# A feed-forward down product by a seven-product block scheme, in a two-layer float32 transformer block on one core

## What is computed

```python
def _swiglu(h, w_gu, w_down):
    gate, up = jnp.split(h @ w_gu, 2, axis=-1)
    return (jax.nn.silu(gate) * up) @ w_down
...
        h = _rms_norm(x, norm_ffn_pre[l])
        y = _swiglu(h, w_gu[l], w_down[l])
        x = x + _rms_norm(y, norm_ffn_post[l])
```

## Time and profile before

| | |
|---|---|
| time, median of 3 runs | 1101.56 us (1101.35 to 1102.26) |
| span of the profiled execution | 1099.9 us |
| PE busy | 1089.6 us (99%) |
| PEld busy | 1014.0 us (92%) |
| DVE busy | 559.5 us (51%) |
| ACT busy | 561.2 us (51%) |
| POOL busy | 670.2 us (61%) |
| DMA | 183.37 MB, mean 167 GB/s |

### The profile page before, as it was taken

The page is one execution under the profiler, slowest core; times in us unless marked ns, Lnnn a source line. Parts: engine busy times, 40 slices in busy tenths (PEclk is TensorE's granted clock), DMA queues, the critical chain, the costliest instruction groups (busy, mean ns, idle before and its releaser), DMA issues.

```text
span 1099.9 us, 19903 instructions
## 1 busy us (share of the span) xinstructions
PE 1089.6 (99%) x8135; PEld 1014.0 (92%) x8138; DVE 559.5 (51%) x1082; ACT 561.2 (51%) x888; POOL 670.2 (61%) x351
## 2 busy tenths in 40 slices
PE   8999999999999999999999999999999999999997
PEld 7999999998898999999999999999989979999996
DVE  6788479354515631223358866793644344212234
ACT  7645864435655544444464567544356554444442
POOL 4876769627673457654377758685378454586442
PEclk9999999999999999999999999999999999999999
DMA  7443544624543655555555444445155255555553
GB/s 291 173 154 135 188 130 163 180 74 170 194 153 125 205 188 186 180 189 180 184 173 173 157 141 164 152 156 163 69 194 194 97 181 178 191 179 187 187 180 112
DMA packets 63337, 183.37 MB, mean 167 GB/s; under 512 B 18576, under 2 KB 19088, under 8 KB 63248
## 3 DMA queue, kind: packets, MB, share of 16 engines
q1 hardware_dynamic: 47936, 172.48, 45.3%
q10 hardware_dynamic: 15312, 9.64, 3.4%
HBM read 179.47 MB, written 2.62 MB: 166 GB/s over the span
## 4 chain that ended last, share of the span: by engine, by line
PE 97%; ACT 1%; DVE 1%; DMA 1%; POOL 0%; issue 0%; SPq 0%; DVEq 0%; ACTq 0%; POOLq 0%
PE psum L494 28%; PE psum L495 27%; PE psum L496 27%; PE psum L658 1%; PE psum L985 1%; PE psum L964 1%; PE psum L699 1%; PE psum L1086 1%; PE psum L588 1%; PE psum L879 1%; PE psum L872 1%; PE psum L754 1%; DMA sb_raw<-weights 1%; PE psum L682 1%; PE psum L843 0%; PE psum L670 0%
## 5 line engine op out<-in xcount | busy, mean ns | idle before, releaser
L391 POOL TENSOR_TENSOR sb_low<-sb_raw,sb_high 128x1024 fp32r<-128x1024 f32 x257 | 616.5, 2413 | 337.3 <-ACT sb_high L381 323.1
L381 ACT ACTIVATE sb_high<-sb_raw 128x1024 fp32r<-128x1024 f32 x322 | 340.1, 1061 | 406.4 <-DMA sb_raw<-weights 361.6
L494 PE MATMUL psum<-sb_h_high,sb_high 128*128 128x256 f32 x1640 | 463.9, 283 | 0.0
L495 PE MATMUL psum<-sb_h_low,sb_high 128*128 128x256 f32 x1640 | 463.3, 282 | 0.0
L496 PE MATMUL psum<-sb_h_high,sb_low 128*128 128x256 f32 x1640 | 462.5, 282 | 0.0
L494 PEld LDWEIGHTS psum<-sb_h_high,sb_high 128*128 128x128 f32 x1640 | 310.3, 189 | 1.8 <-DVE sb_region_c L1879 0.3
L496 PEld LDWEIGHTS psum<-sb_h_high,sb_low 128*128 128x128 f32 x1640 | 308.6, 188 | 0.0
L495 PEld LDWEIGHTS psum<-sb_h_low,sb_high 128*128 128x128 f32 x1640 | 307.7, 188 | 0.9
L391 DVE TENSOR_TENSOR sb_low<-sb_raw,sb_high 128x1024 fp32r<-128x1024 f32 x65 | 85.4, 1314 | 95.4 <-ACT sb_high L381 95.0
L1992 DVE SCALAR_TENSOR_TENSOR sb_conv<-psum,sb_param,sb_conv 128x255 f32<-128x255 f32 (+1 forms) x144 | 58.2, 473 | 37.0 <-ACT sb_conv L1405 36.8
L2248 DVE SCALAR_TENSOR_TENSOR sb_sq<-sb_th,psum 128x512 f32<-128x512 f32 x22 | 15.1, 687 | 110.0 <-ACT sb_th L1610 110.0
(11 more groups left out here) (307 smaller groups left out, 1549.0 us busy)
## 6 DMA issues: line engine op xcount, KB each, us to landing
sb_raw<-weights SPq DMA_DIRECT2D x322, 512.0 KB, 3.2
sb_pre_gain<-pre_gains ACTq DMA_DIRECT2D x6, 512.0 KB, 4.4
sb_post_gain<-post_gains ACTq DMA_DIRECT2D x6, 512.0 KB, 4.5
sb_kx<-mem SPq DMA_DIRECT2D x2, 512.0 KB, 4.4
sb_x<-x SPq DMA_DIRECT2D x1, 1024.0 KB, 10.7
t_dram<-sb_sq ACTq DMA_DIRECT2D x4, 256.0 KB, 2.9
out<-sb_x SPq DMA_DIRECT2D x4, 256.0 KB, 2.0
m_dram<-sb_m ACTq DMA_DIRECT2D x8, 64.0 KB, 2.1
```

The lines of the kernel that those rows point to most:

```text
L381: nc.scalar.activation(high[:, n % HIGHS, :], raw[:, n % RAWS, :], ACT.Copy).then_inc(high_ready, 1)
L391: eng.tensor_tensor(low[:, k, :], raw[:, k, :], high[:, n % HIGHS, :].bitcast(F32), ALU.subtract).then_inc(low_ready[k], 1)
L494: pe.matmul(out, a[0], b[0], start=start, stop=False, **kw)
L495: pe.matmul(out, a[0], b[1], start=False, stop=False, **kw)
```

## The change

The down product of slots 0 to 9 is written as a 2 x 2 block product: A is 256 tokens by 256 hidden features, in blocks A11, A12, A21, A22 of 128 x 128, and B is 256 hidden features by 1024 outputs, in blocks of 128 x 512. Seven block products of sums of blocks replace the eight. Each of the seven has its own PSUM bank over all ten slots, and the four blocks of the result are put together at the end. Slot 10 (`down_end`) still uses the plain form.

- Sums of A: four 128x128 additions on VectorE (`row_sums`). The operands of slot i are now 8 blocks, 128x1024, rounded on ScalarE (`ff_high`) with the remainder on VectorE (`ff_low`).
- Sums of B, from the raw weights: T1 = B12-B11, T3 = B22-B12, T2 = T3+B11, T4 = B21-T2, each 128x512 on VectorE (`first_sum`, `other_sums`), before the raw slots are overwritten by `low`; two roundings of 128x1024 on ScalarE (`sums_high`); one remainder of 128x1024 on GpSimd (T1 and T3) and one on VectorE (T2 and T4, `sums_low`).
- Of the first down half of a slot only B11 is still split, 128x512 (`width`).
- Seven banks are taken, so gate and up share the one that is left: gate block b of slot i lies in the bank's first half and up block b in its second. TensorE goes gate(i,0), up(i,0), then 9 matmuls of down(i-1) (`down_rows`), gate(i,1), up(i,1), then 12 matmuls on the sums (`down_sums`). Gate(i,1) waits until the gated product of block (i,0) has been read out of the bank, gate(i+1,0) until that of (i,1) has. In slot 1 the block (1,1) uses bank 3, and `down_rows(0)`, which opens the seven banks, comes after it.
- All down halves are split on VectorE, all gate and up halves from slot 1 on GpSimd.
- At the end VectorE adds the seven banks (u2, u3, u4, c22, and `whole` four times).

```diff
+UNITS = FF_SLOTS - 1
+P_BANK = {1: 1, 6: 2, 7: 3, 2: 4, 3: 5, 4: 6, 5: 7}
-        + [step for i in range(FF_SLOTS) for step in both("gate", i) + both("up", i) + (both("down", i - 1) if i else [])]
+        + [step for i in range(FF_SLOTS) for step in (both("gate", i) + both("up", i) if i == 0 else
+                                                  [("gate", i, 0), ("up", i, 0)] + (both("down", i - 1) if i > 1 else [])
+                                                  + [("gate", i, 1), ("up", i, 1)] + (both("down", 0) if i == 1 else []))]
...
+                        if (i, b) == (1, 0):
+                            claim("pairs", (dve_ff, ("ff", UNITS, 1)), (0,), False)
+                        elif (i, b) == (1, 1):
+                            claim("pair beside", (dve_ff, ("ff", 1, 1)), (3,), False)
+                        else:
+                            pe.wait_ge(*dve_ff.at(layer, ("ff", i, 0) if b else ("ff", i - 1, 0 if i == 2 else 1)))
...
+                def down_rows(i):
+                    if i == 0:
+                        for p, b in P_BANK.items():
+                            claim(("p", p), (dve_norm, ("x", "ffn", 1, 1)), (b,), False)
                     pe.wait_ge(*dve_part.at(layer, ("ff_low", i)))
+                    w = weights_here(HALF_AT[layer, "down", i, 0])
+                    times(i, 1, A11, w, 0).then_inc(slots.sem, mark(slots, (("down", i), "first")))
+                    w = weights_here(HALF_AT[layer, "down", i, 1])
+                    times(i, 2, A12, w, 0)
+                    times(i, 3, S4, w, 1).then_inc(slots.sem, mark(slots, ("down", i)))
+
+                def down_sums(i):
+                    t = ws_high_t[i % 2][:, :], ws_low_t[i % 2][:, :]
+                    pe.wait_ge(*pool_t.at(layer, ("low", i)))
+                    times(i, 5, S1, t, T1)
+                    times(i, 7, S3, t, T3)
+                    pe.wait_ge(*dve_t.at(layer, ("low", i)))
+                    times(i, 6, S2, t, T2).then_inc(pe_down.sem, mark(pe_down, ("p6", i)))
+                    times(i, 4, A22, t, T4).then_inc(pe_down.sem, mark(pe_down, ("sums", i)))
...
+                for i in range(1, FF_SLOTS):
+                    lows(nc.gpsimd, done, HALF_AT[layer, "up", i, 0] + 1, pool_low)
+                    pool.wait_ge(*act_t.at(layer, ("first", i - 1)))
+                    pool.wait_ge(*dve_t.at(layer, ("t2", i - 1)))
+                    n = (i - 1) % 2
+                    nc.gpsimd.tensor_tensor(ws_low[n][:, 0:2, :], ws_raw[n][:, 0:2, :], ws_high[n][:, 0:2, :].bitcast(F32), ALU.subtract)\
+                        .then_inc(pool_t.sem, pool_t.mark(("low", i - 1)))
+                    lows(nc.gpsimd, done, HALF_AT[layer, "up", i, 1] + 1, pool_low)
...
+                ff_high(0)
+                highs(act, done, HALF_AT[layer, "down", 0, 1] + 1)
+                sums_high(0)
...
+                    lows(V, done, HALF_AT[layer, "down", i - 1, 1] + 1, vector_low)
+                    silu(i, 0)
+                    gated(i, 0)
+                    sums_low(i - 1)
+                    if i < UNITS:
+                        first_sum(i)
...
+                    silu(i, 1)
+                    gated(i, 1)
+                    if i < UNITS:
+                        row_sums(i)
+                        other_sums(i)
+                    ff_low(i)
```

More of the change, by code:

```diff
@@ L400, in vector_low @@
                 return b == 0
-            if part in ("gate", "up", "down") and i not in (3, 4, 5):
+            if part == "up" and i == 0:
                 return n % 2 == 1
+            if part == "down":
+                return True
             if layer > 0 and (part, i, b) in (("xk", 1, 1), ("xk", 2, 0), ("xk", 2, 1)):
@@ L1042, in _, with feature_block @@
                     next_keys(1)
-                def down(i):
-                    pe.wait_ge(*dve_part.at(layer, ("ff_low", i)))
[L1046 to L1052, removed]
+                def feature_block(part, i, b):
+                    if part == "gate":
+                        if (i, b) == (1, 0):
[4 more added lines that the diff above has]
+                            pe.wait_ge(*dve_ff.at(layer, ("ff", i, 0) if b else ("ff", i - 1, 0 if i == 2 else 1)))
+                    wide_half(pair_half(part, i, b), HALF_AT[layer, part, i, b], h).then_inc(slots.sem, mark(slots, (part, i, b)))
@@ L1160, in _ @@
                 by_tile = layer + 1 == DEPTH
[L1161 to L1168, removed]
-                        ff_transposes()
[L1170 to L1176, removed]
+                if by_tile:
+                    first_slot()
+                else:
+                    first_gate()
+                    wide(("up", 0), h, (dve_ff, ("ff", 0)), (1,))
+                for i in range(1, FF_SLOTS):
+                    feature_block("gate", i, 0)
+                    if by_tile and i == 1:
+                        ff_transposes()
+                    feature_block("up", i, 0)
+                    if i > 1:
+                        down_rows(i - 1)
+                    feature_block("gate", i, 1)
+                    feature_block("up", i, 1)
+                    if i == 1:
+                        down_rows(0)
+                    down_sums(i - 1)
+                down_end(UNITS)
         @block.scalar
@@ L1622, in _ @@
+                act.wait_ge(*slots.at(layer, (("down", UNITS - 1), "first")))
+                nc.scalar.activation(s1, psum[:, P_BANK[1], :], ACT.Copy).then_inc(act_ff.sem, act_ff.mark("s1"))
                 post_and_pre_norm("ffn", "down", None, None)
@@ L1861, in postnorm @@
                                                          op0=ALU.mult, op1=ALU.add)
+                            if product == "down" and (c, half) == (0, 0):
+                                between(1, 1)
                             if final:
@@ L1867, in postnorm @@
                             low_parts(ahead((product, LAST[product]), 3 + c))
[L1868 removed]
+                        if between and c == 0 and product != "down":
                             between()
@@ L2262, in _ @@
+                postnorm("ffn", "down", 2, final=True, between=whole)
                 low_parts(FIRST_AT[layer + 1] + 3)
```

210 lines of the change are left out of this document (155 added, 55 removed).

## The result

The changed kernel takes 1257.0 us (median of 4 runs, 1254.1 to 1257.6), the kernel before beside it 1101.9 (1101.4 to 1103.1). The ratio is 1.140 [1.139, 1.142]. The direction was forecast and the size was not: 1187 us, with a range that ended at 1216. The profiled execution has a span of 1255.7 us, 155.8 more than before.

The account below looks back on a forecast made before the run. The prediction took TensorE's own steps as the bound (PE busy 99%). Its terms, -14.0 + 91.7 + 3.0 + 5 = +85.7 on a span of 1099.9, gave 1185.6, with 1.7 for the median 1187 us; range 1140 to 1216.

Parts of the forecast that it names:

- openings, both layers: Start of each layer's feed-forward part: TensorE waits of 9.0 and 5.6 us in slot 1 and smaller ones, 17.5 per layer.
- steady slots, 8 per layer: Each steady slot: TensorE waits 0.53 us ahead of the down rows and 2.64 behind their third matmul, 3.17 in all.
- late loads: Layer 0: loads take 4.3 us to land, not 3.2, delaying T1 and silu by 0.7 us per slot, 5.5 in all.
- ends: Ends of both layers: VectorE's additions of the banks add 2.4 us at the program's end and 0.6 after layer 0.
- Last, the clock: TensorE's clock falls at the openings' long waits and restarts at 1.2 GHz: 5 us, bounds 0 and 11.5.
- the rival of the clock in every slot: Waits of 2.6 us leave TensorE at 1.2 GHz for part of 16 slots: +23 to +46, 1210 to 1233 us; chance 0.13.
- the tie on the port: Steady slot: VectorE's `ff_low` asks at 4.98, ahead of GpSimd's remainder of sums at 5.07, and holds the port to 6.20.
- If VectorE goes first when both ask: Other order in the steady slot: VectorE's lows early, gate(i+1,1) late by 3.3 us; up to 5 us per layer difference.
- The bound of both landings at 4.3: Allowance inside the range for loads landing after 4.3 us in both layers: +10 us.
- The exclusion at the port: VectorE operations with both operands in SBUF and GpSimd's exclude each other, holding the port 2.26, 1.08 or 0.55 us each.
- The rival without the port: The port doesn't count; only the order at the opening costs, 2 x 12.7: +21, 1123 us; chance 0.09.
- the packed port: GpSimd and VectorE pack the port, so a slot takes its sum, 18.0 us: +55, 1157 us; chance 0.20.

Follow-up runs that it names:

- the second experiment: Changed kernel plus 22 matmuls of zeros per slot on TensorE, half ahead of the down rows, half behind their third matmul: 1228.3 us.
- the first experiment: Changed kernel with GpSimd's remainder of the sums made to wait for VectorE's `ff_low` of the same slot: 1183.1 us.
- the run with the tie alone: Changed kernel plus one 128x1 ScalarE copy per slot ahead of the rounding of the sums, so GpSimd asks slightly later: 1217.4 us.
- the fourth experiment: Changed kernel with GpSimd's remainders of gate, up and sums replaced by fills of zeros that read nothing: 1128.4 us.

## Why the prediction was wrong

The sum was +85.7 us; the spans differ by 155.8. Term by term (a wait is counted from one matmul's start to the next, less the step; that the 85.5 also stands in the line of waits above is chance, since that line has two waits more and counts each one 0.16 us shorter):

| term | forecast | measured |
|---|---|---|
| wide matmuls | -14.0 | -14.0 (slots of 16.35 without waits) |
| openings, both layers | 35.0 | 31.8 |
| steady slots, 8 per layer | 51.2, and 5.5 for late loads | 85.5 |
| ends | 3.0 | 5.2 |
| clock | 5 | 47.3 (the remainder) |

**What failed first: the clock.** The step was "Last, the clock", where I let it fall only at the openings, and argued against the rival of the clock in every slot from the earlier trace rows, since it held over 4 us past the last matmul. The runs show the rival's mechanism: with waits of 2.8 and 2.4 us the clock fell in every steady slot. Per slot it cost 23.9 - 16.35 - 5.3 = 2.2 us, 35 us in 16 slots, inside the rival's 23 to 46; the busy TensorE of the second experiment got 29 of the kernel's total back. The rest of the 47.3 is 12 for the 5 that I took. The steps themselves can be added up as a check: what they take above 0.120 and 0.234 us where no wait over 0.1 us stands comes to 36 us in the steady slots, 9 in the two openings and 2 behind the wait at the keys, 47 in all. In the first experiment, where the clock held, the same count gives 0.25 us a slot, so some 4 of the 36 are short waits and not the clock.

The Trainium skill (TensorE: Matmul & The Clock Gate, HAM oscillation — how this bites in real kernels) tells of a kernel that falls back in every round of its loop by waiting some 3 to 5 us for data. The waits forecast here were 0.5 and 2.6 us, so the page did not by itself say that this rival would come true, as I wrote; the measurement decides, and the clock fell with the shorter waits too.

What misled me was one end of a program, taken as evidence on a loop that repeats its wait. The tie isn't needed for it: in the run with the tie alone, whose waits are about those that I forecast, the clock fell as well, and the time was 1217.4, inside the rival's 1210 to 1233 and just past my range.

**What failed second: the tie on the port.** "VectorE's `ff_low` holds the port to 6.20; GpSimd's remainder of sums, asked at 5.07". The distance of 0.09 us was a sum of some ten durations, and came out at -0.01. I did weigh the other order, "If VectorE goes first when both ask", but only for the lows, where it moves little. At `ff_low` it moves everything: the waits of a slot went from 3.17 to 5.3 us, 85.5 in all against 51.2. The added copy on ScalarE, which turns only this order, takes a slot from 23.9 to 21.5 us: 16 x 2.4 = 38 of its 40 us. The waits of a slot went from 5.3 to 3.1, so nearly all of it is wait, and some 2.1 us per slot of the clock's 2.2 stayed.

**Too small: the ends.** For the keys of layer 1 I counted TensorE's 8.6 us of work as cover. Only its first part was: the low of the next half stands behind the additions on VectorE, and TensorE waits 3.5 us against the 0.6 that I took. The program's end was +1.7 for +2.4.

**Too large: late loads.** Loads land in 3.2 us in both layers (medians of 440 to 640 and of 1040 to 1250 us), not in the 4.3 of the earlier trace rows, so the 5.5 us of layer 0 never came. That they land sooner because the slots are longer, and the loads further apart, fits but isn't shown. The bound of both landings at 4.3 was void.

**What held.** The exclusion at the port and its sizes (the 2.83 us of a 512-wide low are 2.28 of GpSimd and 0.55 of its own). The opening: 9.1 to 9.3 and 5.5 us, and in layer 1 the 2.4 of slot 2 after it; in layer 0 that one did not come. The second wait of the steady slot. The 0.70 us per slot saved on TensorE, and that halving the bank of gate and up costs nothing: with GpSimd off the port no wait is left in a slot. The rival without the port, 1123, is near the fourth experiment's 1128, though that run shortens GpSimd's work too. No kernel that keeps the change's instructions comes down to the packed port's 18.0 us per slot: 19.3 was the best.

**Open.** Which waits, how long and how close together, let the clock fall was tried at three points only. The kernel before was not tried with the new opening or balance.

## What to carry to other kernels

Where two engines exclude each other, write down for each meeting who asks first and by how much. If the distance is no larger than the error of the chain that it was worked out from (0.10 us here), price both orders, and fix the cheap one by a wait. When a change gives a busy TensorE waits like these (2.4 us with one of 0.6 ahead of it) in each turn of a loop, price the low clock in each turn, from the first estimate on. An operation saved on the engine that is the bound was worth nothing here as long as the sum of what it added on the shared resource (18.0 us) stood above the new turn (16.4).

## What the runs showed of the hardware

- A lead of 0.01 us decided who had the port. VectorE, going second, took 2.26 us longer (3.48 for 1.22); GpSimd, going second, 1.0 longer (3.40 for 2.40). It came out the same way in all 16 steady slots, and asking 0.09 us later turned it in all 16; in the first slot of each layer, where GpSimd's lead was 0.17, it did not.
- With two waits of 2.8 and 2.4 us and three matmuls between them TensorE was at 1.2 GHz for some 6.8 us of each slot of 23.9 (mean granted clock 0.86). With one of 0.6 and one of 2.4 it fell too, in slots of 21.5 (0.92 in the one shown). One of 1.5 us with shorter ones, in a slot of 19.3, did not, nor did matmuls of zeros in the waits' place.
- GpSimd's fill of 128x2048 bf16 takes 1.80 us and doesn't slow VectorE's operations with two SBUF operands.
